# The weighted sum of value rows with the activations stationary: 512-column streams, sums by token, transposed at the end

## What is computed

```python
def peer_ffn(h, w_pq, sub_keys, u_tab, v_tab):
    ...
    eidx = jnp.take_along_axis(cidx, ti, axis=-1).reshape(n, PEER_HEADS * PEER_TOPK)
    gate = jax.nn.softmax(tv, axis=-1).reshape(n, PEER_HEADS * PEER_TOPK).astype(h.dtype)
    def block(args):
        hx, ei, gt = args
        a = jnp.einsum('tkd,td->tk', u_tab[ei], hx)
        w = gt * jax.nn.gelu(a, approximate=False)
        return jnp.einsum('tk,tkd->td', w, v_tab[ei])
...
        x = x + gt2 * peer_ffn(h2, w_pq[l], sub_keys[l], u_tab[l], v_tab[l])
```

## Time and profile before

| | |
|---|---|
| three runs | 3429.09, 3430.80 and 3432.83 us; median 3430.8 us |
| profiled execution | span 3435.4 us from first to last instruction; the page gives no time for it beside the span |
| busy | TensorE 3014.2 us (88%), its weight loader (PEld) 2849.4 us (83%), VectorE 2246.2 us (65%), GpSimd 1489.5 us (43%), ScalarE 1199.6 us (35%) |
| value stages | about 1253.9 to 1790.6 us and 2885.9 to 3421.5 us of the span: the two last plateaus of TensorE in the page's 40 slices |

### The profile page before, as it was taken

One profiled execution on the slowest core, in us unless ns is written; L12 is line 12 of the kernel. 1 busy time (PEld: TensorE's weight loads), 2 busy tenths in 40 slices (PEclk: granted clock), 3 DMA queues, 4 the chain that ended last, 5 costly groups with the idle time before them and its releaser, 6 DMA issues.

```text
span 3435.4 us, 56066 instructions
## 1 busy us (share of the span) xinstructions
PE 3014.2 (88%) x18256; PEld 2849.4 (83%) x18256; DVE 2246.2 (65%) x5088; ACT 1199.6 (35%) x1619; POOL 1489.5 (43%) x641
## 2 busy tenths in 40 slices
PE   4677699789898999999997769978989899999998
PEld 1365599688888899999986559968888889999998
DVE  0146679999999933333334667999999993444444
ACT  0132335343333333333333233533333333333332
POOL 0042347333343455555544134733434344555554
PEclk8787899899999999999998789989999999999999
DMA  8913205345544477777750320534554447666665
GB/s 334 391 56 136 111 26 161 100 130 174 166 160 167 154 254 245 236 238 245 242 158 2 137 110 26 162 101 126 177 166 160 167 154 249 220 219 223 220 219 168
DMA packets 287521, 591.79 MB, mean 172 GB/s; under 512 B 25908, under 2 KB 210356, under 8 KB 277464
## 3 DMA queue, kind: packets, MB, share of 16 engines
q1 hardware_dynamic: 108064, 386.85, 34.4%
q10 hardware_dynamic: 179384, 204.02, 17.7%
HBM read 483.30 MB, written 107.50 MB: 172 GB/s over the span
## 4 chain that ended last, share of the span: by engine, by line
PE 36%; DVE 34%; issue 15%; DMA 11%; ACTq 2%; ACT 1%; DVEq 1%; POOL 0%; SPq 0%; PEldq 0%
DVE oh L1057 13%; DMA gin<-gate_scratch 9%; PE ps L1417 6%; PE ps L1418 6%; PE ps L1422 6%; DVE oh L1055 4%; DVE wv L1076 3%; PE ps L1316 2%; PE ps L1311 2%; PE ps L1312 2%; DMA wada<-in_wada 2%; PE ps L1368 1%; PE ps L1369 1%; DVE ti L1011 1%; DVE rs L864 1%
## 5 line engine op out<-in xcount | busy, mean ns | idle before, releaser
L1057 DVE TENSOR_SCALAR oh<-cst,iT,gP 128x128 bf16<-128x128 f32 x2304 | 1047.2, 509 | 0.0
L416 POOL TENSOR_TENSOR uring_lo<-uring,uhi 128x1024 fp32r<-128x1024 f32 x256 | 635.9, 2485 | 842.4 <-ACT uhi L427 842.4
L420 POOL TENSOR_TENSOR vring_lo<-vring,vhi 128x1024 fp32r<-128x1024 f32 x256 | 610.7, 2396 | 466.1 <-ACT vhi L427 463.8
L1368 PE MATMUL ps<-hh,uhi 128*128 128x384 f32 x2048 | 739.2, 361 | 3.2 <-ACT uhi L427 3.2
L1369 PE MATMUL ps<-hl,uhi 128*128 128x384 f32 x2048 | 714.0, 349 | 0.0
L1417 PE MATMUL ps<-wvhi,vhi 128*128 128x384 f32 x2048 | 685.6, 335 | 5.8 <-DVE wv_lo L1078 3.8
L1418 PE MATMUL ps<-wv_lo,vhi 128*128 128x384 f32 x2048 | 685.1, 335 | 0.0
L1076 DVE TENSOR_TENSOR wv<-ain,gin 128x768 f32<-128x768 f32 x128 | 286.1, 2235 | 592.8 <-DMA gin<-gate_scratch 413.8
L427 ACT ACTIVATE uhi<-uring 128x1024 fp32r<-128x1024 f32 x256 | 271.5, 1061 | 521.4 <-PE ps L1369 507.8
L1368 PEld LDWEIGHTS ps<-hh,uhi 128*128 128x128 f32 x2048 | 412.7, 202 | 3.6 <-issue 3.6
L1369 PEld LDWEIGHTS ps<-hl,uhi 128*128 128x128 f32 x2048 | 410.0, 200 | 0.0
(11 more groups left out here) (215 smaller groups left out, 3123.4 us busy)
## 6 DMA issues: line engine op xcount, KB each, us to landing
uring<-in_uT SPq DMA_DIRECT2D x256, 512.0 KB, 4.1
vring<-in_vt SPq DMA_DIRECT2D x256, 512.0 KB, 4.2
wada<-in_wada SPq DMA_DIRECT2D x12, 4096.0 KB, 14.8
act_scratch<-aout ACTq DMA_DIRECT2D x128, 384.0 KB, 4.6
gate_scratch<-gst ACTq DMA_DIRECT2D x48, 1024.0 KB, 6.1
ain<-act_scratch ACTq DMA_DIRECT2D x128, 384.0 KB, 3.5
gin<-gate_scratch ACTq DMA_DIRECT2D x128, 384.0 KB, 5.0
wpq<-in_wpq SPq DMA_DIRECT2D x4, 4096.0 KB, 12.2
```

What stands on the lines that cost most here:

```text
L416: sub(uring[s][1][:], uring[s][0][:], uhi[s % 2][:].bitcast(F32), ALU.subtract).then_inc(u_lo, 1)
L420: sub(vring[s][1][:], vring[s][0][:], vhi[s % 2][:].bitcast(F32), ALU.subtract).then_inc(v_lo, 1)
L1057: ins = ts(oh[s][:, k, n, :], iota, iT[:, tok], gP[n][:, tok], ALU.is_equal, ALU.mult)
L1368: mm(out, uhi[s % 2][:, k, :], hh[:, k, :], start=(k == 0), stop=False)
```

## The change

The value stage swaps its operands. PSUM bank 2t + half now holds 128 tokens of block t (TT = 3) by 512 features (DHALF). For each tile, token block and half, TensorE loads 128 columns of wvhi and streams 512 columns of vhi, loads 128 columns of wv_lo and streams them again, then, after the wait for vring_lo, loads wvhi and streams 512 columns of vring_lo: 18 matmuls of 512 columns. Six banks are opened and closed by zero tiles. The sums are then by token, so three steps are new at the end of each layer: ScalarE copies the six banks to ytok (SBUF, where hh was), TensorE transposes them in 24 blocks of 128 by 128 into banks of their own (Y_BANK), three for each chunk, and VectorE's residual waits chunk by chunk for them (ytr_pe) in place of vall_pe.

```diff
--- before.py
+++ after.py
@@ -56,6 +56,8 @@
 Q_BADA, Q_GN, Q_SP, Q_GQK, Q_GSUB, Q_BS, Q_GGV, Q_LAM = 0, 48, 64, 66, 68, 72, 328, 584
 Q_N = Q_LAM + 256
 
+DHALF = 512
+Y_BANK = (0, 2, 4, 6, 7, 1, 3, 5)
 UR = 4
 PAIR = 2
 NTILE = NKEY
@@ -116,7 +118,7 @@
         jT = own("jT", [T])
         gT = own("gT", [T])
         lam = own("lam", [4 + 128])
-        zero = own("zero", [T], BF16)
+        zero = own("zero", [DHALF], BF16)
         st = own("st", [160])
         resid = own("resid", [NB * NS])
         iob = own("iob", [TOPK], BF16)
@@ -200,6 +202,8 @@
         brev = at("brev", [TT, H, NK], HH)
         bias0 = at("bias0", [TT, H, NK], HT)
 
+        ytok = at("ytok", [TT, D], HH)
+
         ps = ctx.enter_context(nc.psum_tensor("ps", [P, 8, 512], F32))
         line_d = nc.dram_tensor("bias_line", (H, DIST), F32, kind="Internal").ap()
         bias_d = nc.dram_tensor("bias_scratch", (P, TT, H, NK), F32, kind="Internal").ap()
@@ -248,6 +252,7 @@
         oh_done, g_pe, g_ev = sem("oh_done"), sem("g_pe"), sem("g_ev")
         v_hi, v_lo, v_used, v_pe, vall_pe = (sem(n) for n in ("v_hi", "v_lo", "v_used", "v_pe", "vall_pe"))
         wmul, wv_hi, wv_lo = sem("wmul"), sem("wv_hi"), sem("wv_lo")
+        ytok_ev, ytr_pe = sem("ytok_ev"), sem("ytr_pe")
 
         block = ctx.enter_context(nc.Block())
 
@@ -767,6 +772,11 @@
                         weigh_pair(i, s)
                 weigh_pair(NPAIR // 2 - 1, 0, load=False)
 
+                act.wait_ge(vall_pe, L)
+                for half in range(2):
+                    for t in range(TT):
+                        copy(ytok[:, t, half * DHALF:(half + 1) * DHALF], ps[:, 2 * t + half, :]).then_inc(ytok_ev, 1)
+
         @block.vector
         def _(dve):
             step = counted(dve)
@@ -1083,9 +1093,9 @@
                     for s in range(2):
                         weigh(i, s)
 
-                dve.wait_ge(vall_pe, L)
                 for k in range(KD):
-                    residual(k, ps[:, k, :], mods[l], 5 * KD)
+                    dve.wait_ge(ytr_pe, KD * l + k + 1)
+                    residual(k, ps[:, Y_BANK[k], :], mods[l], 5 * KD)
 
         @block.tensor
         def _(pe):
@@ -1401,10 +1411,10 @@
                 pe.wait_ge(g_ev, QUADS * L + 2)
                 pe.wait_ge(pick_ev, TT * L)
                 pe.wait_ge(zero_done, 1)
-                for c in (*range(2, KD), 0, 1):
-                    if c < 2:
-                        pe.wait_ge(gelu_done, NTILE * L - 1 + c)
-                    mm(ps[:, c, 0:T], zero[:, 0:P], zero[:, 0:T], start=True, stop=False)
+                for e in range(2):
+                    pe.wait_ge(gelu_done, NTILE * L - 1 + e)
+                for b in range(2 * TT):
+                    mm(ps[:, b, :], zero[:, 0:P], zero[:], start=True, stop=False)
 
                 with pe.Fori(0, NTILE // UR) as i:
                     for s in range(UR):
@@ -1412,18 +1422,28 @@
                         pe.wait_ge(v_hi, UR * i + (s + ub + 1))
                         if s % 2 == 0:
                             pe.wait_ge(wv_lo, 2 * i + (w + pb + 1))
-                        for c in range(KD):
-                            vh = vhi[s % 2][:, c * P:(c + 1) * P]
-                            mm(ps[:, c, 0:T], vh, wvhi[w][:, s % 2, :], start=False, stop=False)
-                            ins = mm(ps[:, c, 0:T], vh, wv[w][1][:, s % 2, :], start=False, stop=False)
+                        for t in range(TT):
+                            tok = slice(t * P, (t + 1) * P)
+                            for half in range(2):
+                                vh = vhi[s % 2][:, half * DHALF:(half + 1) * DHALF]
+                                mm(ps[:, 2 * t + half, :], wvhi[w][:, s % 2, tok], vh, start=False, stop=False)
+                                ins = mm(ps[:, 2 * t + half, :], wv[w][1][:, s % 2, tok], vh, start=False, stop=False)
                         ins.then_inc(v_used, 1)
                         pe.wait_ge(v_lo, UR * i + (s + ub + 1))
-                        for c in range(KD):
-                            ins = mm(ps[:, c, 0:T], vring[s][1][:, c * P:(c + 1) * P], wvhi[w][:, s % 2, :], start=False, stop=False)
+                        for t in range(TT):
+                            for half in range(2):
+                                vl = vring[s][1][:, half * DHALF:(half + 1) * DHALF]
+                                ins = mm(ps[:, 2 * t + half, :], wvhi[w][:, s % 2, t * P:(t + 1) * P], vl, start=False, stop=False)
                         ins.then_inc(v_pe, 1)
+                for b in range(2 * TT):
+                    ins = mm(ps[:, b, :], zero[:, 0:P], zero[:], start=False, stop=True)
+                ins.then_inc(vall_pe, 1)
+
                 for c in range(KD):
-                    ins = mm(ps[:, c, 0:T], zero[:, 0:P], zero[:, 0:T], start=False, stop=True)
-                ins.then_inc(vall_pe, 1)
+                    pe.wait_ge(ytok_ev, TT * (2 * l + c // (KD // 2) + 1))
+                    for t in range(TT):
+                        ins = nc.tensor.transpose(ps[:, Y_BANK[c], t * P:(t + 1) * P], ytok[:, t, c * P:(c + 1) * P], idn)
+                    ins.then_inc(ytr_pe, 1)
 
 
 def buckets():
```

## The result

The changed kernel took **3415.03 us** (median of four runs, 3411.23 to 3418.79) beside 3431.82 us for the kernel before (four runs, 3429.09 to 3440.28): ratio 0.9945, 95% interval 0.9929 to 0.9962, so 16.8 us or 0.55% faster. 6.2 us had been forecast. Timed once more, in experiment 8, the two stood 0.50% apart. The sign of the likeliest case and the range hold; the size of the gain is off by a factor of 2.7, and the time is the one of rival 3.

What follows compares the result with a forecast made beforehand. TensorE was taken to bound the kernel at 8.32 us per pair, the weights' loop close behind at 8.17. Savings of 11.5 us less 5.3 at layer ends gave -6.2 us: 3424.6 us, own range 3421 to 3429, with rivals 3414 to 3438.

Steps and rivals of the forecast that it cites:

- the likeliest case: The forecast's own case for the whole kernel: 3424.6 us, 0.18% faster, chance 0.5.
- rival 3: The weights' loop is less stiff, loads land sooner once TensorE moves, layer 0 gains 10 us: 3416 us; chance 0.06.
- Streams: Value-stage matmuls: 13.3 ns fixed per matmul, so 226.7 ns apart and 4.08 us per tile, from 4.16.
- The loop's own period: Loop making the weights: 8.17 us per pair whatever TensorE does, so layer 1 saves 9.5 us.
- second way: Within a loop round: ScalarE's two vhi copies (2.12 us) and GpSimd's two subtractions (4.75 us), as long as gin's wait.
- Layer 0: Layer 0's value stage: loop already slower because nine 1 MB loads set it back, so only 2.0 us saved.
- Rival 1: Value-stage streams: 512 columns hide the excess, TensorE runs 218 ns per matmul: 3421 us; chance 0.17.
- Rival 2: Value-stage streams: excess grows with columns, 231 ns, no gain, ends cost 5.3 us: 3436 us; chance 0.2.
- Rival 4: Layer 0's nine 1 MB loads each stop TensorE 1 to 2 us and its clock falls: about 3432 us; chance 0.07.
- The ends: End of each layer: copies and transposes delay the first residual 2.4 us; both layers plus square sums cost 5.3 us.
- the square sums: End of layer 0: they start about 2 us later against the residual behind 24 transposes, costing 0.5 us (0 to 1.5).
- the opening tiles: Value-stage opening: six zero tiles wait for both last activations; costs nothing, at most 1.3 us.

Runs made afterwards that it cites:

- experiment 8: The changed kernel, unchanged, timed and traced once more: 3416.64 us, ratio 0.9950 to the kernel before.
- experiment 3: The kernel before with one of a tile's 24 matmuls left out, so TensorE wants 7.97 us per pair: 3400.18 us.
- experiment 5: The changed kernel with two of its 18 matmuls per tile left out, so TensorE wants 7.25 us per pair: 3410.20 us.
- experiment 6: The changed kernel with two of 18 matmuls left out and ScalarE's loads of gin and ain issued ahead of the copy to wvhi: 3302.19 us.
- experiment 1: The kernel before, unchanged, run for a second trace: 3433.37 us, beside 3435.43 for one more run of it in that job.
- experiment 7: The changed kernel with all matmuls and ScalarE's loads of gin and ain issued ahead of the copy to wvhi: 3419.21 us, ratio 0.9955 to the kernel before.

## Why the prediction was off

**Streams: right.** 226.7 ns and 4.08 us per tile were forecast and came. The page of the Trainium skill on TensorE (TensorE: Matmul & The Clock Gate, Back-to-back issue gap) has 2.5 ns over the columns at this clock, as the gap of a matmul by itself; here it is 13.3 ns for the 4-byte format at all three widths, in a stream of loads and matmuls. The same trace has bf16 zero tiles of 512 columns, each 0.38 us long, at (1.24 - 0.38) / 4 = 215 ns from start to start, which agrees with the page's formula. The measurement decides.

**The loop's own period: right for layer 1.** 8.17 us a round "whatever TensorE does": experiments 3 and 5 found 8.1 to 8.3, with TensorE wanting 7.97 and 7.25, and the rows of the changed kernel bear out its second way, by which the product ends when GpSimd lets it. "Whatever TensorE does" holds for this order of ScalarE's lines only: in experiment 6 the loop followed TensorE to 7.25. Layer 1 was forecast 9.5 us shorter. Its stretch got 11.6 shorter, 1.7 of which is the first pair (10.0 us before, 8.3 after), which comes in either length in any kernel (8.4 in experiment 1, 9.9 in experiment 8); without it 62 x 0.16 = 9.9.

**Layer 0: wrong, and this is the step that failed.** The prediction had: "In layer 0 the loop is already the slower one over the stage, since the nine loads set it back each time. TensorE can only draw nearer to it: ... 2.0 us." It gained 12.3 us between the first two traces, and 9.9 between the second ones (experiments 1 and 8), where the prediction had set 4 us as the mark of being wrong: 63 x 0.16 = 10.1 by TensorE's pace, and in the first pair of traces about 2 more by pauses that this execution of the kernel before had and experiment 1 had not. Two errors lie in that sentence.

- The loads don't set the loop back by a fixed price; they take what lead there is. Behind a load that counts, the product ends 12.5 us (after the change) to 12.8 us (experiment 1) after the load's issue, and SyncE issues the load behind a tile of TensorE's, so that moment moves with TensorE. What a load took was 1.1 us at pair 50 of experiment 1 and 0.04 us at pair 56 after the change, where the lead was 0.35 to begin with. Between loads the lead of the kernel before grew by 8.32 - 8.17 = 0.15 us per pair, because TensorE was the slower one. A lead that grows is the mark of a loop with slack, and I read its being eaten every six pairs as a loop without any.
- "The slower one over the stage" is a comparison of means (the prediction expected layer 0's pairs "8.3 to 8.4 us apart on average"), and it can't tell which of the two bounds. Product and TensorE hold each other, so over a stage their means are nearly equal: 8.36 us for both in the first trace, its pauses included. The loop's pace stands only in rounds with no wait for TensorE and no load in them, and the prediction had it from such rounds: 8.17.

Experiment 3 shows it directly: in the kernel before, nothing but a faster TensorE takes layer 0 from 524.3 to 515.0 us. What nine loads cost when the loop has no slack left is between 0.4 us (experiment 5, 514.1 and 513.7 us) and 5.1 us (experiment 3, 515.0 and 509.8 us) per layer; with the slack that the kernel before had it was 0 (experiment 1) to 2.6 us.

**Rivals 1 and 2** fell with the spacing. The Trainium skill, Perfetto Trace Analysis, section Identifying the Most-Contended Engine, judges TensorE by LDWEIGHTS busy time, beside the share of its peak that it reaches: the loader went from full to 83% of the stage and the excess per matmul did not move, so here that share was no sign of a limit.

**Rival 3** had the right time, 3416 us, and was given 0.06. That it came out is in part luck: of its reason, that the transfers would land sooner once TensorE moves, half is true. The moment by which gin lands behind a load does move with TensorE, but its median flight in layer 0's stage was 5.5 us before and 5.4 after. What was put against it, GpSimd's 4.75 us, holds the loop at 8.1 to 8.2 us, and that is no objection: to give layer 0 its full 10 us the loop needs no more than the 8.16 at which TensorE then runs. Rival 4 did not come: one wait of 0.9 us is all that TensorE has in layer 0's stage.

**The ends: nearly right.** 2.4 us per layer were forecast and 1779.25 - 1777.00 = 2.25 measured from the end of the closing matmuls (1775.76 + 1.24) to the residual, in both layers. The 0.5 us for the square sums were nothing (the prediction's "low clock" for them is misread, the granted clock from 1788 to 1800 us of the kernel before is 1.00): from the first residual chunk to the norm's first instruction it is 1791.93 - 1779.25 = 12.68 us, and it was 1803.28 - 1790.60 = 12.68 before. What the opening tiles cost was not isolated; the executions differ by more. The table has 1.8 and 2.0 us at the two ends, each with the last pair's 0.16 us of gain in it. The 2.0 at the end of layer 1 is firm; the 1.8 lies inside the 3 us by which the stretch between the layers varies from one execution to the next.

With layer 0 at its 10.1 us and the ends at 2 x 2.25 the prediction's own sum gives -10.1 - 9.9 + 4.5 = -15.5 us, beside 16.8 measured.

**What stays open.** Why a 4-byte stream has 13.3 ns beside its columns and a bf16 one about 2. Why now and then the product behind a load ends late enough to stop TensorE: 15.0 us behind the load at pair 56 of the first trace, 14.8 at pair 14 of experiment 3 and at pair 38 of experiment 5, and 11.2 to 13.7 at the other loads of the kernels that issue gin behind the copy. Neither trace of the changed kernel has such a one; with its lead of 0.3 us it would pause there too, so that its full gain in layer 0 came in both is not proof against one. And what moves the beginning of the first value stage by up to 14 us between executions.

## What to carry to other kernels

When two loops hold each other, don't compare their means over a stage, which are nearly equal by necessity, nor count which wait is named more often. And when a product waits for a load, look whether its end moves with the landing before you call the load's flight the bound: here it didn't. Follow the distance between the two loops from round to round: if it grows between disturbances, the one ahead has slack, and a disturbance costs only what exceeds the distance. If in doubt, make the follower faster (leave one matmul out) or the leader (issue its load earlier): the one that moves the time is the bound. If neither does alone, as in the changed kernel, the two stand in a tie, and only a run with both tells what lies behind it. A few us of margin that come and go don't matter.

A change of shape that keeps the columns and cuts the number of matmuls is worth the fixed part of each, here 13.3 ns by 6 per tile, and that part can be read from two widths if it stays the same. The price of turning the sums around is the way from the last matmul through the first three copies and transposes to the first residual chunk, 2.25 us a layer; the rest hides behind the residual.

## What had not been expected of the hardware

- The excess of 13.3 ns per 4-byte matmul is the same at 256, 384 and 512 columns (120.0, 173.3, 226.7 ns).
- The loader's busy share did not tell whether loads hold TensorE back: 200 of 200 us before, 165.5 after, in stages where TensorE was full in both and its spacing had the same excess.
- The same product of VectorE is 0.96 or 2.98 us long, and GpSimd's subtraction 2.39 or 3.01, by which of them began a fifth of a microsecond earlier (experiments 6 and 7). The prediction's "it ends when GpSimd lets it" is true where the product is the second of the two, and in the loop of the changed kernel it was in 52 of 53 rounds, whatever the moment at which gin landed.
